# VectorE's first two weight splits of the second mixer, placed behind a residual and behind the last rest piece

## The reference, cut to what matters

```python
def modulate(x, shift, scale):
    return rms_norm(x) * (1.0 + scale) + shift

for i in range(DEPTH):                      # DEPTH = 2
    ...
    xs = xs + ms[2] * os_                   # os_: the mixer's output
    xs = xs + ms[5] * swiglu(modulate(xs, ms[3], ms[4]), w_ffn_in[i], w_ffn_out[i])
```

## Time and profile before

| | us |
|---|---|
| runs, not profiled | 1686.7, 1693.27, 1684.74 (median 1686.7) |
| the profiled execution, device time | 1685.47 |
| its span in the trace | 1683.4 |
| TensorE busy in the span | 1614.8 (96%) |
| VectorE busy | 1124.2 (67%) |
| ScalarE busy | 744.7 (44%) |
| mean granted TensorE clock | 0.989 |

### The profile page before, as it was taken

How to read it: one execution, slowest core, us unless ns; L and a number is a source line. 1 busy time by engine, 2 the same in 40 slices (tenths; PEclk the granted TensorE clock), 3 DMA queues, 4 the chain that set the end, 5 groups by cost and what they waited for, 6 DMA issues and landing times.

```text
span 1683.4 us, 27133 instructions
## 1 busy us (share of the span) xinstructions
PE 1614.8 (96%) x11025; PEld 1485.4 (88%) x11025; DVE 1124.2 (67%) x1922; ACT 744.7 (44%) x1334; POOL 72.3 (4%) x56
## 2 busy tenths in 40 slices
PE   6899996999999999999998999999999999999997
PEld 3589995689998999999998997778999999999997
DVE  4724479677876865865885356844789578487586
ACT  4432464555742532532543543233565245154254
POOL 0000055000000000000000302000000000000000
PEclk9999998999999999999999999999999999999999
DMA  9346314103345545535325203000322322223222
GB/s 320 112 133 213 106 50 149 32 2 100 94 120 163 151 115 161 150 109 167 101 76 169 76 26 103 16 10 13 89 76 70 107 74 85 69 76 101 76 63 88
DMA packets 236838, 168.72 MB, mean 100 GB/s; under 512 B 7925, under 2 KB 232395, under 8 KB 236332
## 3 DMA queue, kind: packets, MB, share of 16 engines
q1 hardware_dynamic: 235796, 166.32, 33.0%
q10 hardware_dynamic: 920, 0.69, 0.2%
HBM read 161.13 MB, written 5.87 MB: 99 GB/s over the span
## 4 chain that ended last, share of the span: by engine, by line
PE 83%; DVE 8%; ACT 3%; DMA 2%; issue 2%; POOL 1%; SPq 1%; DVEq 0%; ACTq 0%
PE ub L1109 6%; PE ub L1111 6%; PE ub L1110 6%; PE ua L1109 5%; PE ua L1491 5%; PE ua L1111 5%; PE ua L1110 5%; PE ua L1493 5%; PE ua L1492 5%; PE ub L1491 5%; PE ub L1493 5%; PE ub L1492 5%; PE pm L1025 2%; PE ua L1339 2%; PE ub L1339 1%
## 5 line engine op out<-in xcount | busy, mean ns | idle before, releaser
L2080 ACT ACTIVATE whi<-weight_sums 128x1024 fp32r<-128x1024 f32 x88 | 93.1, 1058 | 71.6 <-DVE weight_sums L2760 47.1
L1491 PE MATMUL ua<-x_mixed_high,whi 128*128 128x322 f32 x352 | 110.6, 314 | 1.9 <-ACT snap L2153 1.8
L1491 PE MATMUL ub<-x_mixed_high,whi 128*128 128x322 f32 x352 | 111.0, 315 | 0.6 <-ACT snap L2153 0.6
L1493 PE MATMUL ua<-x_mixed_high,wlo 128*128 128x322 f32 x352 | 109.2, 310 | 0.0
L1493 PE MATMUL ub<-x_mixed_high,wlo 128*128 128x322 f32 x352 | 109.2, 310 | 0.0
L1492 PE MATMUL ub<-x_mixed_rest,whi 128*128 128x322 f32 x352 | 109.0, 310 | 0.0
L1492 PE MATMUL ua<-x_mixed_rest,whi 128*128 128x322 f32 x352 | 109.0, 310 | 0.0
L1109 PE MATMUL ub<-hidden_high,whi 128*128 128x384 f32 (+1 forms) x324 | 102.1, 315 | 6.5 <-DVE x L2827 3.5
L2733 DVE TENSOR_TENSOR wlo<-weight_sums,whi 128x1024 fp32r<-128x1024 f32 x88 | 107.3, 1219 | 0.4 <-ACT whi L2080 0.3
L2420 DVE TENSOR_TENSOR wlo<-raw,whi 128x2048 fp32r<-128x2048 f32 (+1 forms) x31 | 57.9, 1869 | 70.6 <-ACT whi L1799 63.4
L1109 PE MATMUL ua<-hidden_high,whi 128*128 128x384 f32 (+1 forms) x324 | 101.0, 312 | 1.9 <-DVE x L2827 1.9
(11 more groups left out here) (683 smaller groups left out, 5118.5 us busy)
## 6 DMA issues: line engine op xcount, KB each, us to landing
raw<-in_w_ffn_in SPq DMA_DIRECT2D x88, 512.0 KB, 5.4
mod_late<-in_w_mod SPq DMA_DIRECT2D x24, 1024.0 KB, 5.3
raw<-in_w_ffn_out SPq DMA_DIRECT2D x48, 384.0 KB, 4.6
modw<-in_w_mod SPq DMA_DIRECT2D x14, 1024.0 KB, 5.5
raw<-in_w_in_even SPq DMA_DIRECT2D x10, 1024.0 KB, 7.8
raw<-in_w_in_odd SPq DMA_DIRECT2D x7, 1024.0 KB, 5.6
mod_first<-in_w_mod SPq DMA_DIRECT2D x5, 1024.0 KB, 12.2
mod_tail<-in_w_mod SPq DMA_DIRECT2D x4, 1024.0 KB, 6.3
```

What stands on the lines that cost most here:

```text
L1491: pe.matmul(dst, wh[:, c], xh, start=first, stop=False, skip_group_check=True)
L1493: ins = pe.matmul(dst, wl[:, c], xh, start=False, stop=last, skip_group_check=True)
L2080: act.activation(ring(whi, g, w), src, ACT.Copy).then_inc(g_hi, 1)
```

## The change

VectorE's two weight splits of the second mixer's tiles 0 and 1 are moved. The split of tile 0 was behind the sixth residual (m = 5) and ahead of rest piece 5; it now stands behind the seventh residual (m = 6) and ahead of rest piece 6. The split of tile 1 was behind the seventh residual and ahead of rest piece 6; it now stands behind the loop, after rest piece 7 and the last addition to ssq. ScalarE's, TensorE's and SyncE's programs are the same as before.

```diff
                     fast_out_unit(e, m)
                     if m + 4 < KD:
                         out_rest(e, m + 4)
-                    if m in (5, 6):
-                        w_rest(U_ODD + m - 5, (U_ODD + m - 5) % 2, 2048)
+                    if m == KD - 2:
+                        w_rest(U_ODD, U_ODD % 2, 2048)
                     dve.wait_ge(x_up, x_before(e) + m + 1)
                     scaled_rest(hin_b, m, m % 2)
                     add_tile(2, m)
+                w_rest(U_ODD + 1, (U_ODD + 1) % 2, 2048)
```

## The result

| | before | changed |
|---|---|---|
| median of 10 runs each, us | 1685.7 (1684.26 to 1696.11) | 1677.97 (1676.61 to 1681.82) |
| ratio, 95% interval | | 0.995 (0.9936 to 0.9964) |
| profiled execution: device time, span | 1685.47, 1683.4 | 1681.82, 1679.8 |

The changed kernel is faster, by 0.5%. The time lies in the predicted range (1677.6 to 1684.0), 2.0 us under the predicted 1680.0. The most likely outcome was given as "within 0.5%", called about what a measurement can tell from no change, and that is where the prediction went wrong: the interval is clear of no change. Whether the gain is more than 0.5% isn't settled by it (0.36% to 0.64%).

What follows compares the result with a forecast made beforehand. TensorE bounds the kernel, with a hole in the second mixer's first unit; pauses 1.31 and 3.26, restart 0.10 and low clock 1.46 sum to 6.1 us. Forecast 1680.0 us, 8-in-10 range 1677.6 to 1684.0.

Steps and rivals of the forecast that it cites:

- within 0.5%: Whole kernel: time changes by less than 0.5% (8.4 us), called about what a measurement can tell; chance 0.83.
- What bounds it, and the mechanism: Second mixer's first unit: TensorE waits twice for VectorE's rest pieces, VectorE and ScalarE queued behind each other; 6.1 us removable.
- Residual 7: VectorE: would wait for TensorE alone and run 899.51 to 900.65, gaining 3.6 us.
- residual 8: VectorE: its unit ends at 904.72, so it would run 904.8 to 905.9 instead of starting at 911.92.
- Split 0: VectorE, weight tile 0: would run about 900.6 to 902.9 without waiting, 1.7 us of slack before unit 0.
- split 1: VectorE, weight tile 1: would run 908.9 to 911.2, last, and cost nothing of its 2.29 us.
- Rivals 1 to 4: Pieces still late, chance 0.07; transfer replaces the pause, 0.04; clock falls without the pause, 0.03; edit does nothing, 0.02.
- The Trainium skill's gap between matmuls: TensorE step in unit 0: formula gives 818 ns and a 7.2 us gain; prediction kept the trace's 0.887 us.
- the low clock behind the long pause: TensorE, eighth step and sum over partitions in unit 0: 0.88 + 0.58 = 1.46 us saved.
- pauses and restart: TensorE in unit 0: pause 1.31 us, slower restart 0.10, pause 3.26, all to disappear.
- The base: Whole kernel: profiled 1685.47 less 6.1 gives 1679.4, the runs' median gives 1680.6; the middle, 1680.0, was taken.
- The chance of 0.15 for a gain over 0.5%: Whole kernel: a time of 1678.3 us or less, taken as scatter at the low edge; chance 0.15.

Runs made afterwards that it cites:

- e3: Kernel before with only the split of tile 0 moved, behind the seventh residual; against before: ratio 0.9962, median 1679.95 us.
- e6: Changed kernel plus two needless splits of weight tile 1 between residual 8 and rest piece 7; against before: ratio 0.9977, median 1680.48 us.
- e1: Kernel before, no edit, timed against itself: ratio 1.0 (0.9986 to 1.0014), medians 1686.23 and 1685.18 us.
- e7: Kernel before, no edit, a single profiled execution: device time 1692.6 us, 22.81 us from unit 0 to unit 1.
- e5: Changed kernel plus three needless splits of weight tile 1 between residual 8 and rest piece 7; against before: ratio 0.9984, median 1683.23 us.
- e2: Changed kernel measured again, no further edit, against the kernel before: ratio 0.9964 (0.9948 to 0.998), median 1678.46 against 1685.18 us.

## Why the prediction came out as it did

**What bounds it, and the mechanism: right.** Each step showed. Residual 7 from 904.74, counted from unit 0's start 5.04 us before it (899.51 predicted, 5.05 before); residual 8 at +0.20 (+0.2 predicted); no pause; clock 1.00; unit 1 at +15.24 (+15.26 predicted). Split 0 came at -3.99 (-4.0) and split 1 at +4.33 (+4.3). Nobody waited for the moved splits. Rivals 1 to 4 didn't happen.

**The Trainium skill's gap between matmuls** ("TensorE: Matmul & The Clock Gate", section "Back-to-back issue gap"), worked out for this step, was an estimated 818 ns, and an earlier unit 1. The page gives the formula for an isolated gap and says itself that a stream of weight loads and matmuls departs from it, which the prediction left out. The trace of after says 0.887 again, with no wait anywhere in the unit, so keeping the row was right. The same page's warning about short idles ("A second HAM failure mode: psum-queue depth-cycling") is about frequent ones, and no run here tests that: e3 and e6 had one pause each in this unit, of 0.93 and 0.67 us idle, and a clock of 1.00 behind it.

**The term that was mis-sized: the clock.** The prediction put 1.46 us for the low clock behind the long pause, the value of its single trace. Over six executions the first unit of before is 21.80 on the mean; less 15.24 and the 4.67 of pauses and restart that leaves 1.9 us, 1.7 to 1.8 in four of them and 2.9 in one. This makes the gain 6.4 to 6.6. It was known from the earlier trace rows that the term is a matter of the clock; the forecast gave it no width.

The traces show what sets it: half of the time that TensorE works at 0.50. The first line is of the kernel before in the prediction's trace, at the end of the long pause, the other three of e1, where TensorE works again from 916.94:

```profile
914.50:915.40 0.90, 0.00 (x0) 0.00 (x0) 0.90 (x4) 0.88 (x2) 0.00 (x0) 0.75 1.16 306
```
```profile
916.00:917.00 1.00, 0.06 (x1) 0.06 (x1) 1.00 (x4) 0.98 (x2) 0.00 (x0) 1.00 1.17 303
917.00:918.00 1.00, 1.00 (x6) 1.00 (x7) 0.62 (x1) 0.62 (x1) 0.00 (x0) 0.80 1.33 235
918.00:921.00 3.00, 3.00 (x9) 2.20 (x9) 0.00 (x0) 0.46 (x1) 0.00 (x0) 0.50 1.14 307
```

In the prediction's trace the clock was down before TensorE started again at 915.44, so a part of the low clock fell on an idle engine and cost nothing; from the earlier trace rows some 2.9 us of work stood under it, half of which is the 1.46. In e1 it went down after the restart, and 3.4 us of work stood under it: 1.7. In e7 it was some 6.0 us, from 922.77 on (windows at the end): 3.0 by this, 2.9 by the first unit.

**The base: 1.2 us taken half.** The prediction started from the middle between the profiled time less 6.1 and the median of three less 6.1. Over all timed runs with the medians 1685.7, 1685.18 and 1685.18, before lies at 1685.2 (1685.3 with the twelve of e1, whose median is 1686.23), so the median of three, 1686.7, was 1.5 high, and the profiled 1685.47 near the truth. 1685.2 less 6.4 to 6.6 is 1678.6 to 1678.8; the two measurements of the changed kernel gave 1677.97 and 1678.46.

**The step that failed: from the gain to the outcome.** The sum gave 6.1 us, 0.36%, with the whole place laid out to a tenth. The prediction then set beside it a bound of 0.5%, 8.4 us, as "about what a measurement of this kernel can tell from no change", a figure that no row or run before it gives, and so called the outcome "within 0.5%", with 0.83. The measured interval, 0.9936 to 0.9964, reaches 0.14% to either side, and e1 shows the same 0.14% for the kernel against itself. Against that a gain of 6.1 us is more than twice what can be told, so its own sum should have led it to forecast a clear gain. The three runs that it had, 1684.74 to 1693.27, show how far single executions scatter, which isn't how far a median can be off. The second fault is the size: 1680.0 was forecast and 1677.97 measured, and the clock term above accounts for 0.3 to 0.5 us of these 2.0, the base for 0.9, the rest is scatter or open. The chance of 0.15 for a gain over 0.5% can't be faulted from these runs: the gain of 6.6 us (0.39%) lies 1.8 us short of the bound, and of the two ratios one is at it (0.995) and one inside (0.9964).

Why the first measurement gave 7.7 us in the medians and the second 6.7 is not settled in detail. Both intervals (0.9936 to 0.9964 and 0.9948 to 0.998) reach 6.6 us, ratio 0.9961, and the scatter of the first 70 us and of the two later pauses, 8 and 2.5 us in the table, is more than enough for the difference. That it is chance alone is argued from these, not shown.

No experiment pointed to a kernel better than the changed one: no wait of TensorE is left at this place, and moving split 1 alone is 0.23 us behind it in the traces.

## What to carry to other kernels

When two in-order engines feed each other, a wait for the partner's by-product (here a weight's high part) must not stand ahead of the work that the partner itself waits for; put it where its own consumer's deadline is, and write the deadlines down. Lay the new order out from the durations of the old trace: it was right to 0.02 us for the changed kernel and to about a tenth in e3, e5 and e6. But read several executions before pricing a clock effect, and test the resolution of a comparison with the kernel against itself before calling a gain too small to see.

## What the runs showed of the hardware

A pause of 3.1 us (idle of TensorE, all six executions of before, and 2.99 in e5) was each time followed by a stretch at half clock (1.2 of 2.4 GHz), pauses of 1.14, 0.93 and 0.67 us in the same unit never. Pauses of 2.3 to 2.8 us near 1187 and of 2.0 near 1644 were followed by it in some executions and not in others of the same kernel. How much of TensorE's work falls under the low clock differs too. These windows are of e7, the execution with 22.81:

```profile
922.00:924.00 2.00, 1.23 (x4) 1.23 (x5) 1.46 (x4) 1.44 (x2) 0.00 (x0) 0.50 1.26 261
924.00:926.00 2.00, 2.00 (x7) 1.39 (x6) 0.00 (x0) 0.00 (x0) 0.00 (x0) 0.50 1.11 289
926.00:928.00 2.00, 2.00 (x8) 1.81 (x7) 0.00 (x0) 1.07 (x3) 0.00 (x0) 0.50 0.92 299
928.00:930.00 2.00, 2.00 (x13) 2.00 (x12) 0.00 (x0) 1.90 (x2) 0.00 (x0) 0.80 0.01 4
```

In the first 60 us, where TensorE works in short pieces, whether the clock is low costs several us. The first two lines are of the changed kernel's first profile (unit 0 at 909.78), the next two of e2, the same program (904.40):

```profile
35.00:40.00 5.00, 5.00 (x24) 2.02 (x23) 1.18 (x2) 1.50 (x3) 0.00 (x0) 0.50 1.07 367
40.00:45.00 5.00, 5.00 (x8) 1.84 (x6) 4.70 (x9) 2.00 (x2) 0.00 (x0) 0.50 0.65 173
```
```profile
35.00:40.00 5.00, 5.00 (x27) 2.09 (x27) 4.31 (x7) 2.88 (x4) 0.00 (x0) 1.00 1.07 366
40.00:45.00 5.00, 5.00 (x26) 1.88 (x25) 4.65 (x8) 2.51 (x4) 0.00 (x0) 1.00 0.67 177
```

From 61 us on the same instructions of VectorE start 6.4 us later in the first of these two executions than in the second, and at unit 0 they are still 5.4 apart, nearly the whole gain of this change. That the clock is the cause is read from these windows and not shown by a run. Only the distance inside the changed stretch could be compared trace against trace.
